# Eight modulation chunks summed on GpSimd, and all weights stored chunk by chunk, in a two-block transformer kernel

## The reference, cut to what matters

```python
cond_x = jax.nn.silu(c)
cond_c = jax.nn.silu(c_ctx)
for l in range(DEPTH):
    mod_x = (cond_x @ w_mod[l] + b_mod[l])[:, None, :]
    mod_c = (cond_c @ w_mod[l] + b_mod[l])[None, None, :]
    sh1x, sc1x, g1x, sh2x, sc2x, g2x = jnp.split(mod_x, N_MOD, axis=-1)
    ...
    hc = modulate(rms_norm(xc, norm1_g[l]), sh1c, sc1c)
    yc, s_f, s_b = token_mixer(hc, w_in[l], w_out[l], conv_w[l], ...)
    xc = xc + g1c * yc
    xc = xc + g2c * peer_ffn(hc2, peer_wq[l], peer_subkeys[l], peer_u[l], peer_v[l])
    ... the same for x, with mod_x
```

## Time and profile before

| what | value |
|---|---|
| time, median of 3 runs | 3438.97 us (3438.48 to 3441.64) |
| profiled execution, its time | 3438.76 us |
| profiled execution, its span | 3437.0 us |
| mean granted PE clock | 0.907 |
| PE busy | 2768.4 us (81%) |
| DVE busy | 2433.8 us (71%) |
| POOL busy, all of it issuing transfers | 959.2 us (28%) |
| mean transfer rate over the span | 336 GB/s |

### The profile page before, as it was taken

How to read it: one execution, slowest core, us unless ns; L and a number is a source line. 1 busy time by engine, 2 the same in 40 slices (tenths; PEclk the granted TensorE clock), 3 DMA queues, 4 the chain that set the end, 5 groups by cost and what they waited for, 6 DMA issues and landing times.

```text
span 3437.0 us, 38166 instructions
## 1 busy us (share of the span) xinstructions
PE 2768.4 (81%) x13522; PEld 1759.4 (51%) x13522; DVE 2433.8 (71%) x4596; ACT 1200.3 (35%) x2832; POOL 959.2 (28%) x809
## 2 busy tenths in 40 slices
PE   6997799676877786777996879766697789989898
PEld 5876468342533232234674645222242456969696
DVE  4666978868789894758687658889746764556554
ACT  3112431223334442434223123333324354543263
POOL 0003224334344443454341034544335100000000
PEclk9998899887999987898997989898898899999999
DMA  8976899899999999999997689999999663555454
GB/s 305 366 282 273 359 359 412 328 372 402 423 421 413 421 407 402 397 413 404 395 371 288 246 352 421 427 427 416 403 409 412 268 226 135 203 196 191 164 200 142
DMA packets 278322, 1155.91 MB, mean 336 GB/s; under 512 B 20127, under 2 KB 21344, under 8 KB 179392
## 3 DMA queue, kind: packets, MB, share of 16 engines
q0 software_dynamic: 113344, 813.02, 57.7%
q1 hardware_dynamic: 163064, 334.76, 26.5%
q10 hardware_dynamic: 1736, 5.90, 0.4%
HBM read 1149.48 MB, written 4.13 MB: 336 GB/s over the span
## 4 chain that ended last, share of the span: by engine, by line
PE 40%; DMA 21%; DVE 17%; issue 15%; ACT 3%; SPq 2%; POOL 1%; DVEq 0%; POOLq 0%; ACTq 0%
DMA arena<-in_peer_uv,arena 13%; PE ps L1482 7%; PE ps L1044 5%; PE ps L1046 5%; PE ps L1045 5%; DVE arena L3044 4%; PE ps L1399 4%; PE ps L1446 2%; DVE arena L3057 2%; DMA ring<-in_peer_wq 2%; PE ps L1502 2%; DMA ring<-in_w_in 2%; PE ps L1248 2%; PE ps L1556 1%; PE ps L1311 1%
## 5 line engine op out<-in xcount | busy, mean ns | idle before, releaser
L1482 PE MATMUL ps<-arena 128*128 128x512 f32 x1996 | 1083.7, 686 | 405.1 <-ACT arena L2118 385.0
L3368 POOL DMA_INDIRECT arena<-in_peer_uv,arena x732 | 893.1, 1220 | 1280.5 <-PE ps L1482 826.1
L1482 PEld LDWEIGHTS ps<-arena 128*128 128x128 f32 x1996 | 405.7, 214 | 1009.4 <-ACT arena L2118 609.1
L3044 DVE CUSTOM_DVE_ANT_0 arena<-arena,hA 128x1024 f32<-128x1024 f32 x476 | 572.9, 1223 | 203.5 <-DMA arena<-in_peer_uv,arena 197.2
L2113 ACT ACTIVATE arena<-arena 128x1 f32<-128x1 f32 x768 | 155.5, 202 | 1364.5 <-DVE arena L3044 1359.3
L3044 DVE CUSTOM_DVE_ANT_0 arena<-arena,hB 128x1024 f32<-128x1024 f32 x256 | 310.2, 1226 | 142.4 <-DMA arena<-in_peer_uv,arena 136.7
L2504 DVE TENSOR_TENSOR w_lo<-ring,w_hi 128x1024 fp32r<-128x1024 f32 x220 | 264.9, 1223 | 146.5 <-ACT w_hi L1888 140.4
L3057 DVE SCALAR_TENSOR_TENSOR arena<-arena 128x1024 f32<-128x1024 f32 x227 | 290.7, 1281 | 42.8 <-ACT arena L2115 39.7
L1888 ACT ACTIVATE w_hi<-ring 128x1024 fp32r<-128x1024 f32 x220 | 230.4, 1059 | 208.7 <-DMA ring<-in_w_mlp_out 87.8
L1044 PE MATMUL ps<-hT_hi,w_hi 128*128 128x256 f32 x992 | 286.2, 289 | 15.3 <-DVE hT_lo L2512 15.2
L1046 PE MATMUL ps<-hT_hi,w_lo 128*128 128x256 f32 x992 | 283.1, 285 | 0.0
(11 more groups left out here) (365 smaller groups left out, 3433.3 us busy)
## 6 DMA issues: line engine op xcount, KB each, us to landing
arena<-in_w_mod SPq DMA_DIRECT2D x52, 1024.0 KB, 9.3
ring<-in_w_in SPq DMA_DIRECT2D x16, 2048.0 KB
ring<-in_w_mlp_in SPq DMA_DIRECT2D x64, 512.0 KB, 5.2
ring<-in_w_mlp_out SPq DMA_DIRECT2D x64, 512.0 KB, 5.9
ring<-in_peer_wq SPq DMA_DIRECT2D x12, 2048.0 KB
ring<-in_w_in SPq DMA_DIRECT2D x44, 512.0 KB, 7.7
hA<-in_w_mod SPq DMA_DIRECT2D x13, 1024.0 KB, 11.5
ring<-in_attn_w_qkv SPq DMA_DIRECT2D x24, 512.0 KB, 6.1
```

The source lines that it names most:

```text
L1482: mm = pe.matmul(ps[:, 6 + c, :], place(j)[:, 0:P], place(j)[:, D + c * CW:D + (c + 1) * CW], start=start, stop=stop)
L3044: dve.tensor_tensor_reduce(row, row, peer_buf[p][:, t, :], 1.0, 0.0, ALU.mult, ALU.add, dots[:, column(j):column(j) + 1]).then_inc(dot_don ...
L3368: pool.indirect_dma_start(place(j), None, A["peer_uv"], at).then_inc(uv_full[slot_of[j]], 16)
```

## The change

Two things are done.

First, modulation chunks 16 to 23 go to a stream of their own on POOL. For a half, POOL multiplies each of four k-tiles by the condition value of its partition (four 128x512), adds two tiles to two (one 128x1024), then adds what is left into one half of `acc` (one 128x512 for the first half, two for the second). PE needs four narrow products with a matrix of 1/128 to sum over the partitions, in place of 64; DVE multiplies by 128 and adds the bias in `late_io`. POOL's chunks have two half buffers, slot 8 of `uv` and `xs`; PE's chunks 4 to 15 turn over three (0, 1 and 7). PE reads a POOL chunk's sums at the place named in the new `PLACES`, and POOL may not overwrite the sums of chunk n - 2 before that. Stores of batches 0 to 3 move from POOL's queue to SP's. ACT waits for the stores of batch 5 before it uses the memory that `late_io` lies in. Chunk 23 is no longer done in the middle of the L1248 products.

Second, all weights are laid out on the host as [chunk, partition, k-tile, column], so that a partition's share of a chunk is one piece of 16 KB (8 KB for a half, 4 KB for a quarter).

```diff
         def chunked(w, c0=0):
-            v = w.rearrange("(k p) n -> p k n", p=P)
-            return lambda c: v[:, :, bass.ds(c * CW + c0 * CW, CW)]
-        def chunked_deep(w):
-            v = w.rearrange("(g k p) n -> g p k n", k=KT, p=P)
-            return lambda c: v[c // 2, :, :, (c % 2) * CW:(c % 2 + 1) * CW]
+            return lambda c: w[c0 + c]
...
         PRO = 24
+        POOL_BATCHES = (4, 5)
+        ON_POOL = 16
         HALF = 4 * CW
         half_buf = [uv[:, s, :] for s in range(EARLY_SLOTS)] + [b[:, :, :].rearrange("p t d -> p (t d)") for b in (xs, hA)]
+        half_buf.append(uv[:, EARLY_SLOTS, :])
         half_buf = [b.rearrange("p (k n) -> p k n", n=CW) for b in half_buf]
         def half_of(n, h):
             if n < 4:
                 return (2 * n + h) % EARLY_SLOTS
-            return (0, 1)[h] if n % 2 == 0 else (6, 7)[h]
+            if n < ON_POOL:
+                return (0, 1, 7)[(2 * (n - 4) + h) % 3]
+            return (8, 6)[h]
         half_used = collections.Counter()
...
-        PLACES = [[4], [5], [6, 7]] + [[8, 9], [10, 11], [12, 13], [14, 15], [16, 17], [18], [19], [20, 21], [22], []]
+        holder_before, half_holder = {}, {}
+        for n in range(PRO):
+            for h in range(2):
+                holder_before[n, h] = half_holder.get(half_of(n, h))
+                half_holder[half_of(n, h)] = n, h
+        PLACES = [[4], [5], [6], [7, 16], [8, 17], [9, 18], [10, 19], [11, 20], [12, 21], [13, 22], [14], [15, 23], []]
+        EARLY_ORDER = [*range(4), *itertools.chain(*PLACES)]
+        order_no = {n: i for i, n in enumerate(EARLY_ORDER)}
+        POOL_STEPS = 13
+        def pool_sums(n):
+            return acc[:, n % 2 * CW:(n % 2 + 1) * CW]
+        def half_read(n, h):
+            if n < ON_POOL:
+                return mod_half, 2 * order_no[n] + h + 1
+            return pool_step, POOL_STEPS * (n - ON_POOL) + (6 if h == 0 else POOL_STEPS)
+        def bias_at(batch):
+            if batch in POOL_BATCHES:
+                return pool_bias, 64
+            return bias_in[batch % 2], 32 * ((batch if batch < 4 else batch - 2) // 2 + 1)
...
             def bias(tile, batch):
-                if batch >= 2:
-                    sp.wait_ge(*stored_at(batch - 2))
+                if batch not in POOL_BATCHES:
+                    sp.wait_ge(*stored_at(batch - (4 if batch in (6, 7) else 2)))
                 for who in range(2):
                     sp.dma_start(spread(tile, batch % 2, who), A["b_mod4"][batch // 3, batch % 3 * 4 * CW:(batch % 3 + 1) * 4 * CW
                                                                            ].rearrange("(c q f) -> q c f", c=4, q=COLS)
-                                 ).then_inc(bias_in[batch % 2], 16)
+                                 ).then_inc(bias_at(batch)[0], 16)
+            def store(batch):
+                sp.wait_ge(mod_taken, order_no[4 * batch + 3] + 1)
+                for who in range(2):
+                    sp.dma_start(batch_rows(batch // 3, batch % 3, who),
+                                 spread(mod_io, batch % 2, who)).then_inc(early_stored[batch % 2], 16)
...
+                        mod_half_load(n, h)
+            def mod_half_load(n, h):
+                b = half_of(n, h)
+                if half_turn[n, h] > 1:
+                    sp.wait_ge(*half_read(*holder_before[n, h]))
+                elif b == 7:
+                    sp.wait_ge(tr_done, 4)
+                src = A["w_mod4"][n // 12, n % 12, :, 4 * h:4 * h + 4]
+                sp.dma_start(half_buf[b], src).then_inc(mod_full[b], 16)
...
             in0 = L_in[0]
             chunk(in0, 0, 0, 0)
             chunk(in0, 1, 0, 1)
-            mod_load(4, 5)
+            bias(late_io, 4)
+            bias(late_io, 5)
+            mod_load(4, 16)
+            mod_half_load(5, 0)
             chunk(in0, 2, 0, 2)
-            mod_load(6)
+            store(0)
+            bias(mod_io, 2)
+            mod_half_load(5, 1)
+            mod_load(6, 17)
             chunk(in0, 3, 0, 3)
-            mod_load(7)
+            mod_load(18, 7)
             chunk(in0, 4, 0, 4)
-            bias(mod_io, 2)
-            mod_load(8, 9, 10, 11)
+            mod_load(8, 19, 9)
             chunk(in0, 5, 0, 5)
+            store(1)
             bias(mod_io, 3)
-            mod_load(12, 13, 14, 15)
+            mod_load(20, 10, 11)
             chunk(in0, 6, 0, 6)
-            bias(mod_io, 4)
-            mod_load(16, 17, 18, 19)
-            chunk(in0, 7, 0, 7)
             modulated(1)
             load_rows("r_c0")
-            bias(mod_io, 5)
-            mod_load(20, 21, 22, 23)
+            mod_load(21, 12, 13)
+            chunk(in0, 7, 0, 7)
+            store(2)
+            mod_load(22, 14, 15, 23)
+            sp.wait_ge(mod_half, 2 * order_no[15] + 2)
             sp.wait_ge(ring_done, in0.g0 + 6 + 3)
             sp.dma_start(out_weights(0, 1), L_out[0].src(1)).then_inc(out_full[1], 16)
             chunk(L_wq[0], 0, 0, 0)
-            sp.wait_ge(mod_half, 2 * 22 + 2)
             sp.dma_start(out_weights(0, 0), L_out[0].src(0)).then_inc(out_full[0], 16)
+            store(3)
...
                 for n in chunks:
+                    i = order_no[n]
                     if n >= 4:
-                        pe.wait_ge(mod_taken, n - 1)
-                    bank, at = (6 + n // 3, n) if n < 4 else (6 + n % 2, 0)
+                        pe.wait_ge(mod_taken, i - 1)
+                    bank, at = (6 + n // 3, n) if n < 4 else (6 + i % 2, 0)
+                    if n >= ON_POOL:
+                        pe.wait_ge(*half_read(n, 1))
+                        for q in range(COLS):
+                            mm = pe.matmul(ps[q * 32:q * 32 + 1, bank, 0:P], mean_mat[:, 0:1],
+                                           pool_sums(n)[:, q * P:(q + 1) * P], start=True, stop=True)
+                        mm.then_inc(mod_half, 2)
+                        continue
...
-                pe.wait_ge(mod_taken, PRO - 1)
+                pe.wait_ge(mod_taken, PRO)
...
-                early(PRO - 1)
...
+                act.wait_ge(*stored_at(5))
                 take_states(0)
...
+            def add_sums(batch, c, bank):
+                if c % 4 == 0:
+                    dve.wait_ge(*bias_at(batch))
+                for q in range(COLS):
+                    own, cols = slice(q * 32, q * 32 + 1), slice(c % 4 * P, (c % 4 + 1) * P)
+                    ins = dve.scalar_tensor_tensor(late_io[own, batch % 2, cols], ps[own, bank, 0:P], float(P),
+                                                   late_io[own, batch % 2, cols], ALU.mult, ALU.add)
+                ins.then_inc(mod_taken, 1)
...
-            for batch in range(PRO // 4):
-                pool.wait_ge(mod_taken, 4 * batch + 4)
+            pool.wait_ge(cond_ready, 1)
+            upto = 0
+            for n in range(ON_POOL, PRO):
+                for h in range(2):
+                    rows_ = half_buf[half_of(n, h)]
+                    pool.wait_ge(mod_full[half_of(n, h)], 16 * half_turn[n, h])
+                    for k in range(4):
+                        pool.tensor_scalar(rows_[:, k, :], rows_[:, k, :], condS[:, 4 * h + k, X:X + 1], None, ALU.mult
+                                           ).then_inc(pool_step, 1)
+                    upto += 4
+                    pool.wait_ge(pool_step, upto)
+                    pool.tensor_tensor(rows_[:, 0:2, :], rows_[:, 0:2, :], rows_[:, 2:4, :], ALU.add).then_inc(pool_step, 1)
+                    if h == 0 and n >= ON_POOL + 2:
+                        pool.wait_ge(mod_half, 2 * order_no[n - 2] + 2)
+                    for first, second in [(rows_[:, 0, :], rows_[:, 1, :])] if h == 0 else [(pool_sums(n), rows_[:, k, :]) for k in range(2)]:
+                        upto += 1
+                        pool.wait_ge(pool_step, upto)
+                        pool.tensor_tensor(pool_sums(n), first, second, ALU.add).then_inc(pool_step, 1)
+                    upto += 1
+            for batch in POOL_BATCHES:
+                pool.wait_ge(mod_taken, order_no[4 * batch + 3] + 1)
                 for who in range(2):
                     pool.dma_start(batch_rows(batch // 3, batch % 3, who),
-                                   spread(mod_io, batch % 2, who)).then_inc(early_stored[batch % 2], 16)
+                                   spread(late_io, batch % 2, who)).then_inc(pool_stored, 16)
             pool.wait_ge(mod_half, 2 * PRO)
...
+    def chunks(w):
+        v = w.reshape(w.shape[:-2] + (-1, KT, P, w.shape[-1] // CW, CW)).swapaxes(-4, -2)
+        return v.reshape(w.shape[:-2] + (-1, P, KT, CW))
...
+    for k in ("w_mod4", "w_in", "w_out", "peer_wq", "attn_w_qkv", "attn_w_out", "w_mlp_in", "w_mlp_out", "hy_w_in", "hy_w_out"):
+        r[k] = chunks(r[k])
```

43 lines of the change are left out of this document (20 added, 23 removed).

## The result

The changed kernel takes 3509.97 us in the median of 4 runs (3504.34 to 3512.98), the kernel before 3440.06 us beside it (3438.48 to 3441.64): ratio 1.0201, 95% interval 1.0184 to 1.0219. It is 70 us slower. The prediction said 3444 us, range 3416 to 3470, so its range does not hold the time. Slower was its likeliest direction, with a chance of 0.44, though 3444 itself lies within the 6.9 us that it counted as no change. The profiled execution has 3508.79 us and a span of 3506.9 us.

The account below looks back on a forecast made before the run. PE was taken to bound the first mixer and transfers the gather stretches. 3438.8 us + 26 (early stage) - 23 (layout) = 3442, written as 3444 us because errors lean to more; range 3416 to 3470.

Parts of the forecast that it names:

- early stage: First mixer, where PE sets the end: waits of 47 us against gains of 20.7 us, +26 us in all.
- Price of a POOL chunk: One modulation chunk on POOL takes 16 us: 8.2 us at DVE's times, times 1.56, plus seven semaphore waits.
- (a) Level 0: SP holds `w_in` chunk 4 behind chunk 18's second half, so level 0 begins at 119 us: 16 us of PE wait.
- (b, c) Waits for POOL: PE waits for POOL's sums: about 6 us at place 8, 10 at place 9, 10 at place 11 (chunks 21 to 23).
- The narrow products: On PE, the four products replacing a chunk's 64 take under 0.3 us, so eight chunks take 12.5 us off PE.
- A further 2 to 3 us go ... in loads for three buffers in place of four: At places 3 to 6 of the early stage, loads cost 2 to 3 us more with three buffers.
- The clock: In the early stage, PE runs at a lower granted clock after waits of 10 us and more: 2 us.
- POOL and DVE block each other: Slower rival, early stage: POOL waits while DVE runs, 5 us more a chunk (21 each), 3462 us in all; chance 0.2.
- Layout: Larger pieces on q1 cost 8% less: 16 us in the gather stretches, 7 us of `peer_wq` wait; -23 us.
- POOL is near DVE's speed: Faster rival, early stage: a POOL chunk takes 9 to 10 us, early stage +5, total 3419 us; chance 0.2.

Follow-up runs that it names:

- no_products: The changed kernel with POOL's 64 products left out, so chunks 16 to 23 lack the condition: 3467.09 us, ratio 1.0079.
- three_buffers: layout_only with PE's chunks 4 to 22 going round three half buffers in place of four: 3462.70 us, ratio 1.0049.
- layout_only: The kernel before with the new memory layout of the weights alone, POOL only issuing transfers: 3434.26 us, ratio 0.9972; run again 0.9962.
- side_memsets_b: layout_only with 92 idle fills of 128x512 on POOL between its stores: 3436.61 us, ratio 0.9966.
- side_products_b: layout_only with 92 idle products of a 128x512 tile with a column on POOL between its stores: 3434.72 us, ratio 0.9962.
- fills_for_products: The changed kernel with POOL's four products of each half replaced by fills that take as long: 3496.08 us, ratio 1.0152.
- later_no_products: The changed kernel with `w_in` chunk 4 issued ahead of chunks 18 and 7, biases 2 and 3 loaded later, POOL's products left out: 3461.75 us, ratio 1.0051.
- one_product: The changed kernel with `w_in` chunk 4 issued ahead of chunks 18 and 7, and one two-tile 128x2048 product for four on POOL: 3504.09 us, ratio 1.0173.

## Why the prediction was wrong

It was right in direction and in three mechanisms (`w_in` chunk 4 held back on SP, PE waiting for POOL at the late places, the layout cheaper by the MB), and wrong by 66 us in their sizes and in what it left small. Some 52 us of it lie in the early stage (+26 forecast, 78.6 measured at the issue gap), 10 to 13 in the layout.

PE's time in the changed kernel adds up to that. Its waits grow by 45.7 us for POOL's sums, 20.4 for level 0 (23.8 against 3.4), 14.8 for its own modulation loads (18.1 against 3.3) and 7.3 for the split of `w_in` chunk 3; its busy time grows by 2.6. That makes the 90 us by which the stretch ends later. Behind it 11 us come back: 6.2 of the wait for `w_out`, 1.9 of chunk 23, and 3.0 because L1248's products ran slower before, right behind that wait.

- **Price of a POOL chunk: mis-sized.** 16 us taken, some 24 measured. The factor came from two issue rows (1.56) on top of DVE's times. For sums it was not far off: 1.27 to 1.29 us undisturbed against DVE's 0.684, and 2.34 to 2.39 against 1.22, factors of 1.9; the Trainium skill's 1.96 (GPSIMD Engine Reference, §3, the comparison of the per-element rates) agrees. For the product it was: 1.54 us undisturbed, against the 0.46 read between DVE's rows, a factor of 3.4. A factor taken from one form does not carry to another. The products cost 42 us (no_products).
- **(a) Level 0: right mechanism, too small.** 119 us forecast, 129.74 measured; chunk 4's load issued near 111 us in place of 89.5. The whole error is POOL's: it ended its chunk 17 at 109.4, not 99 (24.7 us in place of 16, from 84.76). From there on the forecast held: the last quarter of `w_in` chunk 4 was there at 125.10, 15.7 us later (15.6 forecast), and level 0 began 4.6 us after that, as before. Undoing the order gave back 14 us of the 16 forecast.
- **(b, c) Waits for POOL: too small.** 26 us forecast, 45.7 measured, at the three places named: 15.5 us for chunk 21 (6 forecast), 10.7 for chunk 22 (10) and 19.5 for chunk 23 (10).
- **A hold-up that the sum lacks.** The prediction has SP hold back one load of PE's for POOL, `w_in` chunk 4. PE's own chunk 10 stands behind POOL's chunk 20 in the same way and costs the wait of 15.1 us shown above; the sum had nothing for it.
- **The narrow products: a little too small.** 0.3 us a chunk taken, 0.51 measured (4.08 us for eight), so eight chunks take 10.8 us off PE and not 12.5.
- **"A further 2 to 3 us go ... in loads for three buffers in place of four": the step that failed most in a run of its own.** three_buffers measured it at 28 us. I had read the waits for loads of before (some 3 us in all) and took it that they would grow a little. Transfers were at 1.02 in the second window, with as many halves in flight as the buffers allowed; that row should have warned that a buffer less is transfer time lost each time round. In the changed kernel itself the missing buffer hardly shows as a wait of PE for a load (3 us beside the 15.1); where it shows is on SP, whose load of chunk 15's last half waits for PE's use of chunk 14 until 268.16 us, with POOL's chunk 23 behind it. How much of the 28 us is in the 70 isn't shown.
- **The clock: mis-sized.** 2 us taken. PE is busy 163.1 us from 49 to 307 in the changed kernel and 160.5 us from 49 to 217 before (windows summed), with 9.3 us of work less (seven chunks out of this stretch, 13.4 us, the narrow products in, 4.1): some 12 us more for the same work, at a granted clock of 0.80 where it was 0.99. That is about what the eight chunks took off PE. From 49 to 217 us the granted clock is 0.98 in layout_only, 0.90 in three_buffers and 0.84 in the changed kernel, each with more waits of PE than the one before it.
- **The rival "POOL and DVE block each other": it was part of the answer.** It named +5 us a chunk, and 3462 us by itself; the chunk was longer by 2 to 3 us (24 against 21.6 undisturbed), while DVE's two rows grew by 40% and 49%, 24 us in all. The Trainium skill, SBUF, State Buffer (Who interferes with whom), which stood beside this rival, is borne out: fills on POOL, which read nothing, left DVE's two-input rows at 1221 and 682 ns (side_memsets_b), products did not (side_products_b), nor did sums (no_products). The share of the products' reading is about 17 us (fills_for_products); the sums' share wasn't measured.
- **Layout: right by the MB, half the size in time.** In the first gather stretch q1 moved 72.53 MB at 11.3% of 1545 us in the changed kernel, 2.41 us a MB against 2.62: 8% less, as taken. The time gained alone is 10 to 13 us, not 23. Between 217 and 360 us DVE's wait for gathers rises from 5.6 to 11.1 us beside the faster load. PE's 12.9 us for `peer_wq` are gone, but its waits at the gathers' sums are 407.7 and 413.5 us in the two runs of the layout where they were 385.0; that the one turned into the other is likely, not shown.
- **A slip in a rival.** "POOL is near DVE's speed" with +5 early makes 3421 us, not 3419. Nothing rests on it.

The ledger, in ratios: the changed kernel stands 2.3% over layout_only. Leaving out POOL's products takes 1.2% off (of it 0.5% by reading beside DVE); `w_in` chunk 4's place takes 0.4% off with the products there and, with the biases, 0.3% without them; 0.8% are left (later_no_products). That is the size of the fourth buffer alone (three_buffers, 0.8%), but as PE still waits for POOL there, the equality may be chance.

Open: whether the layout gives its 10 us in the changed kernel too, as the ratios are exact to 0.2% only; how much of the loss is the fourth buffer and how much POOL's sums once its products are gone; and how the 12 us of clock divide among the causes of the waits.

## What to carry to other kernels

Count the buffers that a helper engine takes away as well as its speed: here one half buffer less for the main loop cost 28 us with nobody else involved. Give an engine only as much as it does in the time between two uses, load its data where it is sure to be done with the last, and let nothing that another engine needs queue behind its loads: four chunks so placed, with all buffers left to PE, cost nothing where eight cost 70 us. In a queue that is served in order, look for every load behind the helper's, not only the first. And price an operation on another engine form by form; in these runs GpSimd and VectorE delayed each other where both read SBUF.

## What was not expected of the hardware

- On POOL a 128x512 product with a column takes 1.54 us, one of two tiles 1.22 us: the form with fewer inputs is the slower.
- What DVE's 128x512 product (684 ns alone) takes depends on what POOL runs: 804 ns beside products of one tile alone (side_products_b), 1022 in the changed kernel, 1085 with nothing on POOL but its sums of two tiles (no_products), 1819 beside two-tile products of 128x2048, 3.7 to 4.2 us each (one_product).
- Short fills on POOL (128x512) do not touch DVE's two-input operations (682 ns, side_memsets_b). Long ones (128x2048, 1.81 us) take DVE's 128x256 product with a column from 346 to 928 ns (fills_for_products); beside the short ones it stayed at 344.
